# Key lookup in PEER routing: the keys written out by ScalarE before VectorE multiplies by them

## The reference, cut to what matters

```python
sv, si = lax.top_k(s, PEER_TOPK)                       # 16 best of 128, for each half
comb = sv[:, :, 0, :, None] + sv[:, :, 1, None, :]
cv, ci = lax.top_k(comb.reshape(N, PEER_HEADS, PEER_TOPK * PEER_TOPK), PEER_TOPK)
i1 = jnp.take_along_axis(si[:, :, 0], ci // PEER_TOPK, axis=-1)
i2 = jnp.take_along_axis(si[:, :, 1], ci % PEER_TOPK, axis=-1)
expert = i1 * PEER_NKEYS + i2
gate = jax.nn.softmax(cv, axis=-1)
```

## Time and profile before

| what | value |
|---|---|
| median of 3 runs | 3561.27 us (3556.86 to 3562.12) |
| time of the profiled execution | 3564.63 us |
| its span, first to last instruction | 3563.0 us |
| PE busy | 3114.4 us (87%) |
| DVE busy | 2311.0 us (65%) |
| ACT busy | 904.1 us (25%) |
| POOL busy | 1446.0 us (41%) |
| mean granted TensorE clock | 0.949 |

### The profile page before, as it was taken

One profiled execution on the slowest core, in us unless ns is written; L12 is line 12 of the kernel. 1 busy time (PEld: TensorE's weight loads), 2 busy tenths in 40 slices (PEclk: granted clock), 3 DMA queues, 4 the chain that ended last, 5 costly groups with the idle time before them and its releaser, 6 DMA issues.

```text
span 3563.0 us, 46587 instructions
## 1 busy us (share of the span) xinstructions
PE 3114.4 (87%) x17171; PEld 2346.7 (66%) x17171; DVE 2311.0 (65%) x4881; ACT 904.1 (25%) x1256; POOL 1446.0 (41%) x1188
## 2 busy tenths in 40 slices
PE   8899969444677557999999999999999999999996
PEld 1466634222454446888887888888888888888884
DVE  1233218999988976777776777776777775444445
ACT  0111111000666782222222122222222222221222
POOL 0001001555444556555554555555545543222224
PEclk9999989777899888999999999999999999999998
DMA  9611242666121329999998999999999997655654
GB/s 359 174 60 67 72 157 94 229 225 224 73 101 78 159 118 357 336 334 324 337 331 314 335 326 336 335 322 335 341 325 337 329 328 258 213 195 208 212 199 177
DMA packets 305763, 858.03 MB, mean 241 GB/s; under 512 B 25360, under 2 KB 108816, under 8 KB 303840
## 3 DMA queue, kind: packets, MB, share of 16 engines
q0 software_dynamic: 151344, 551.09, 43.0%
q1 hardware_dynamic: 154189, 305.27, 24.8%
q10 hardware_dynamic: 108, 0.22, 0.0%
HBM read 793.34 MB, written 63.15 MB: 240 GB/s over the span
## 4 chain that ended last, share of the span: by engine, by line
PE 59%; POOL 1%; issue 1%; DVE 1%; DMA 0%; ACT 0%; DVEq 0%
PE y_ps L1724 25%; PE a_ps L1705 24%; PE picked_ps L1742 7%; PE uT_ps L1692 3%; POOL shared L1446 0%; POOL rstd_d L1450 0%; DMA shared<-in_peer_u,ids 0%; POOL shared L1398 0%; POOL quad L1408 0%; DMA quad<-in_peer_v,idsT 0%; DVE h_lo L1640 0%; POOL quad L1446 0%; DVE uT_lo L1528 0%; DVE quad L1652 0%; DVE shared L1569 0%
## 5 line engine op out<-in xcount | busy, mean ns | idle before, releaser
L1408 POOL DMA_INDIRECT quad<-in_peer_v,idsT x512 | 533.4, 1042 | 518.2 <-PE picked_ps L1742 367.5
L1398 POOL DMA_INDIRECT shared<-in_peer_u,ids x384 | 444.5, 1158 | 640.5 <-DVE acts L1569 593.0
L1557 DVE TENSOR_TENSOR shared<-shared,y_ps 128x512 f32<-128x512 f32 x640 | 439.2, 687 | 340.2 <-PE y_ps L1724 312.1
L1705 PE MATMUL a_ps<-h_hi,uT_lo 128*128 128x320 f32 x2048 | 643.1, 314 | 1.7 <-DVE h_lo L1640 1.7
L1705 PE MATMUL a_ps<-h_hi,uT_hi 128*128 128x320 f32 x2048 | 633.1, 309 | 0.0
L1705 PE MATMUL a_ps<-h_lo,uT_hi 128*128 128x320 f32 x2048 | 633.1, 309 | 0.0
L1724 PE MATMUL y_ps<-v_hi,m_lo 128*128 128x512 f32 x1280 | 510.7, 399 | 11.0 <-DVE shared L1557 8.5
L1724 PE MATMUL y_ps<-v_lo,m_hi 128*128 128x512 f32 x1280 | 504.3, 394 | 0.0
L1724 PE MATMUL y_ps<-v_hi,m_hi 128*128 128x512 f32 x1280 | 501.6, 392 | 0.0
L1569 DVE CUSTOM_DVE_ANT_0 shared<-shared 128x1024 f32<-128x1024 f32 x384 | 464.6, 1219 | 22.3 <-DMA shared<-in_peer_u,ids 17.2
L1705 PEld LDWEIGHTS a_ps<-h_hi,uT_lo 128*128 128x128 f32 x2048 | 385.3, 188 | 7.2 <-issue 2.1
(11 more groups left out here) (172 smaller groups left out, 4220.1 us busy)
## 6 DMA issues: line engine op xcount, KB each, us to landing
shared<-in_peer_u SPq DMA_DIRECT2D x128, 512.0 KB
v_all<-in_peer_v SPq DMA_DIRECT2D x128, 512.0 KB
gate_blocks<-dense SPq DMA_DIRECT2D x10, 4096.0 KB, 11.7
gates<-gate_blocks SPq DMA_DIRECT2D x64, 640.0 KB
w_ada<-in_w_ada SPq DMA_DIRECT2D x12, 2048.0 KB, 11.0
x_in<-in_x_prompt SPq DMA_DIRECT2D x16, 512.0 KB, 4.1
quad<-in_peer_v,idsT POOLq DMA_INDIRECT x512
shared<-in_w_in SPq DMA_DIRECT2D x8, 768.0 KB, 12.5
```

Of the source, the lines that this page charges most:

```text
L1398: pool.indirect_dma_start(out=rows[n % 4], out_offset=None, in_=u_table, in_offset=bass.IndirectOffsetOnAxis(ap=ids[:, t, slot:slot + 1], ...
L1408: pool.indirect_dma_start(out=quads[half][q], out_offset=None, in_=v_table, in_offset=bass.IndirectOffsetOnAxis(ap=idsT[:, t, token:token ...
L1557: nc.vector.tensor_tensor(part, part, y_ps[n % RING][:, :], ALU.add).then_inc(S.y_free, 1)
L1705: last = nc.tensor.matmul(a_ps[n][:, 0:GROUP], lhs[s][:, k, :], rhs[:, k, tok], start=k == 0 and m == 0, stop=k == KD - 1 and m == 2)
```

## The change

A buffer `key_wide` is added that holds, for the eight heads of one half, each key written out 16 times. ScalarE fills it (`widen_keys`), for the first half at b = 6 and for the second half at b = 14 of the same period. VectorE multiplies by this buffer. Since both halves share one buffer, ScalarE's second filling waits for VectorE's first product (`first_keyed`), and VectorE's second product waits for the second filling. The first product now stands ahead of `rows(15)`, the second behind it. VectorE's wait behind the writing of `best_key` is dropped.

```diff
+        key_wide = sbuf(nc, mem, "key_wide", [P, HEADS, TOPK, TOPK], BF16)
...
+            def widen_keys(t, s):
+
+                act.wait_ge(S.best_key, t + 1)
+                if s:
+                    act.wait_ge(S.first_keyed, t + 1)
+                else:
+                    wait(act, S.keyed, t)
+                nc.scalar.activation(key_wide[:, :, :, :],
+                                     key4[:, :, s, :].rearrange("p h (a o) -> p h a o", o=1)
+                                     .to_broadcast([P, HEADS, TOPK, TOPK]), ACT.Copy).then_inc(S.key_wide, 1)
...
+                    if choose is not None and b == 6:
+                        widen_keys(choose, 0)
                     if choose is not None and b == 12:
                         act.wait_ge(S.shifted, choose + 1)
                         nc.scalar.activation(soft[:, :, :], soft[:, :, :], ACT.Exp).then_inc(S.exp, 1)
+                    if choose is not None and b == 14:
+                        widen_keys(choose, 1)
...
-                own.mark(nc.vector.tensor_copy(best_key[:, :, :], best_at[:, :, :]))
+                wait(dve, S.key_wide, t * 2)
+                nc.vector.tensor_copy(best_key[:, :, :], best_at[:, :, :]).then_inc(S.best_key, 1)
                 rows(3)
-                own.settle()
...
+                own.settle()
+                dve.wait_ge(S.key_wide, t * 2 + 1)
+                nc.vector.tensor_tensor(hit[:, 0:HEADS], hit[:, 0:HEADS], key_wide[:, :, :, :], ALU.mult)\
+                    .then_inc(S.first_keyed, 1)
                 rows(15)
-                own.settle()
-                for s in range(2):
-                    own.mark(nc.vector.tensor_tensor(
-                        hit[:, s * HEADS:(s + 1) * HEADS], hit[:, s * HEADS:(s + 1) * HEADS],
-                        key4[:, :, s, :].rearrange("p h (a o) -> p h a o", o=1)
-                        .to_broadcast([P, HEADS, TOPK, TOPK]), ALU.mult))
+                dve.wait_ge(S.key_wide, t * 2 + 2)
+                own.mark(nc.vector.tensor_tensor(hit[:, HEADS:HP], hit[:, HEADS:HP], key_wide[:, :, :, :], ALU.mult))
+                dve.wait_ge(S.first_keyed, t + 1)
                 own.settle()
```

More of the change, by code:

```diff
@@ L702, in routing @@
                                "scores_used shifted exp gate_ready keyed slotsT_ps slotsT left_hot left "
-                               "right_hot right place_ps placed out0 out1 dve expert picked row_in used "
+                               "right_hot right place_ps placed out0 out1 best_key key_wide first_keyed dve expert picked row_in used "
                                "u0 u1 u2 u3 u4 u5 u6 u7")
@@ L930, in _ @@
             own = Order(dve, S.dve)
-            PER_TILE = 141
+            PER_TILE = 139
             dve.wait_ge(S.iota, 2)
```

## The result

| | before | after |
|---|---|---|
| median of 6 runs, us | 3561.32 (3556.86 to 3564.86) | 3534.97 (3530.5 to 3539.57) |
| ratio to before | 1 | 0.9925, 95% interval 0.9915 to 0.9935 |
| predicted | | 3551.2 (3546 to 3559) |

The sign was right, the size was not, and the question is where the other 16 us came from. (The two profiled executions lie 31.1 us apart, spans 3563.0 and 3531.9; single executions of either kernel scatter by 8 to 9 us.)

A forecast was written before the change was run, and what follows sets the result against it. PE bounds the experts, DVE tiles 1 to 4, ACT tiles 5 to 7 from batch 4, DVE tile 8. Terms 0.1 - 8.1 - 0.3 - 1.85 = -10.1 us gave 3551.2 us, range 3546 to 3559.

The forecast's parts named there:

- Prices of products and copies: Each new product on DVE takes 1.22 us instead of 2.28, each added copy on ACT 1.9 us.
- The two rivals on them: Copies slow at 4.25 us, sum +15.9 us (chance 0.07); products stay at 2.28 us, together +8.9 us (chance 0.04).
- the slow copies: Rival on ACT's copies: 4.25 us each, sum +15.9 us, 3577 us; by the skill's rule 3.5 us each (chance 0.07).
- The two other rivals: Tiles 5 to 7 keep ACT's full 1.75 us, sum -4.5 (0.22); tiles 5 to 8 all save 2.0, sum -16 (0.05).
- Tile 0, +0.1: In tile 0 the second copy must follow the exponentials, so the first add starts 0.1 us later.
- Tiles 1 to 4, -8.1: From L1032's start to the first add 9.01 us become 7.00, 2.02 saved four times, second copy hidden by row products.
- Tiles 5 to 7, the work in them, -0.3: DVE's 2.1 us saved go into ACT's delay of 1.75 and waits for POOL: -0.1 us a tile, periods unchanged within 1 us.
- the bound of -0.85: Tiles 5 to 7: the gain if POOL is out of the way and the copy alone is waited for.
- Tile 8, -1.85: In tile 8 the comparison L1032 no longer stands behind POOL's `right`, and ACT leads: 1.85 us saved, bounds 0 and -2.0.

The follow-up runs named there:

- e3: The changed kernel with both copies and all waits kept, but the two products read best_key repeated as before: 3551.85 us, 0.9963 of before.
- e1: The kernel before with fifteen idle increments ahead of routing on VectorE, its loop moved by 14 instructions: 3544.96 us, 0.9946 of before.
- e5: The changed kernel once more, unaltered: 3536.52 us, 0.9926 of before.
- e10: The kernel before with VectorE's loop over tiles 5 to 7 written out: 3544.32 us, 0.9948 of before.
- e12: The changed kernel with the change in tiles 0 to 4 alone, the old order and repeated key in tiles 5 to 8: 3534.31 us, 0.9922 of before.
- e8: The changed kernel with its loop moved by 48 more instructions on VectorE: 0.9919 of before.
- e11: The changed kernel with VectorE's loop over tiles 5 to 7 written out: 3537.09 us, 0.9927 of before.

## Why the prediction was wrong

**The step that failed** is that for tiles 5 to 7. It took their periods as filled with the work of DVE, ACT and POOL, and said that they stay unchanged within 1 us (91.4, 93.7 and 88.0 us became 83.7, 83.7 and 83.4). They held 19.2 us of DVE at a standstill for code, and the change removed 18.5 of them by moving the loop. With about 7.5 us of its own work that makes 26.0 of the 26.4 us measured. The sum had no term for the place of the code, and no rival did; the range could not reach there. The row was in the profile of before: idle time of a `MAX8` that nothing ended. The worth of the work itself was forecast well: by the tiles below it is +0.3 - 7.3 - 2.8 = -9.8 us in the profiles, and 7.2 to 7.5 us by the times, where 10.1 was said. That the sign of the whole was right says little, since most of the gain came from what the sum did not hold.

**Prices of products and copies:** right, 1.22 and 1.95 us (1.22 and 1.9 taken). The two rivals on them fall. (For the 2.28 of the old product the overlap had to be added to the 4.49 before halving, not taken off; the figure is right, 2.29 in e3.) The 1.9 was in part luck: it was drawn through two rows as plain copies, and that of 1024 elements, `squares`, is a squaring. The rule of the Trainium skill that went with the slow copies ("Vector Engine (DVE) Microarchitecture Reference", 5.2), which the page measured on DVE, does not carry over to this copy on ACT: with each element read 16 times it took 1.89 us in tile 0, where ACT has nothing else beside it, and not 3.5.

**The two other rivals** fall by the tiles: tiles 5 to 7 do not keep ACT's whole delay (+5.3 us), and ACT's delay is not absorbed either (2.0 saved in each of tiles 5 to 8).

**Tile 0, +0.1:** +0.3 against e1, and as described: the second product waits 2.13 us for its copy, which stands behind the exponentials.

**Tiles 1 to 4, -8.1:** -7.3 against e1 (1.8, 1.8, 1.8, 2.0). The second copy is hidden by the two row products.

**Tiles 5 to 7, the work in them, -0.3:** -1.8 in the mean of the profiles above (-3.6 for the first profile against e1, -0.6 for e5's). The mechanism was as described, but for the last wait, which is ACT's copy and not POOL. End of tile 6 after, answering to the earlier trace rows:

```profile
1053.73 2.28 DVE L1048 TENSOR_TENSOR work<-rank,iota_rank 128x4096 bf16<-128x4096 bf16 x1
1054.53 3.77 POOL L840 TENSOR_TENSOR right<-right_hot,gateT 128x1024 f32<-128x1024 bf16 x1 [1.27 <-PE place_ps L1190]
1056.14 3.25 DVE L1055 TENSOR_TENSOR work<-work,key_wide 128x2048 bf16<-128x2048 bf16 x1
...
1060.06 2.76 POOL L840 TENSOR_TENSOR right<-right_hot,gateT 128x1024 f32<-128x1024 bf16 x1 [1.77 <-DVE right_hot L1102]
1060.42 2.07 ACT L889 ACTIVATE key_wide<-best_key 128x2048 bf16<-128x2048 bf16 x1
...
1062.53 1.38 DVE L1059 TENSOR_TENSOR work<-work,key_wide 128x2048 bf16<-128x2048 bf16 x1 [1.94 <-ACT key_wide L889]
```

The first product takes 3.25 with POOL in front (3.5 said). The second starts 8.80 behind the comparison's start (9.28 worked out), the copy being what ends last, not POOL: the bound of -0.85 that the prediction named. How much later ACT's first copy makes the comparison start (1.75 said) can't be read from one pair of tiles: it starts 69.5 us into tile 6 here, and 69.7 in e1. In the nine tiles 5 to 7 of e1, e10 and e12 it starts 68.0 to 69.7 us into the tile, in the twelve of the changed kernel, e5, e8 and e11 69.5 to 72.7: 1.5 later in the mean. From its start to the first add it is 10.2 us for 12.4. Together that is some -0.7 a tile.

**Tile 8, -1.85:** -0.7 in the first profile and in e5's. End of tile 8 after, answering to the earlier trace rows:

```profile
1217.09 2.39 DVE L1044 CAST rank<-ranks 128x128 bf16<-128x128 f32 x1
...
1220.61 2.28 DVE L1048 TENSOR_TENSOR work<-rank,iota_rank 128x4096 bf16<-128x4096 bf16 x1
...
1228.68 2.11 DVE L1059 TENSOR_TENSOR work<-work,key_wide 128x2048 bf16<-128x2048 bf16 x1 [1.21 <-ACT key_wide L889]
```

The comparison is free of `right` (2.28 us for 4.50), as said. But it starts 69.3 us into the tile where it was taken to start as before, at 67.7, and that is most of what is missing. It is not ACT that holds DVE there: the cast just ahead runs beside `right` of batch 13 and takes 2.39 us (0.21 before). In e8 the comparison starts 68.2 in, and the tile takes 84.30. Why DVE meets `right` at that instruction stays open. Ahead of its first add the second product then waits 1.21 us for the copy.

## What to carry to other kernels

Before pricing an edit inside or ahead of a long loop, look at the first instruction behind the loop's jump: idle time put down to "issue", with packets on an instruction queue, was code being fetched here, and 14 instructions more ahead of the loop, of whatever kind, switched it off. Judge such an edit beside a copy of the old kernel with its loop moved by as many idle instructions; else the place of the code is taken for the worth of the work (here 18.5 of 26 us). What helped here was to write the loop out for that engine, to move it, or to keep the large stores away from the jump.

## What the runs showed of the hardware

A loop of some 310 instructions on DVE was kept or fetched anew, five packets of 8 KB a round, by its place: fetched at 0 and 110 instructions from before's place, counted within 128, and kept at 14 and 62, with either kernel's work. The packets wait behind the data: 3.1 and 1.4 us a jump with quiet queues, 7.4 and 2.2 behind a store of 4 MB. Code without jumps was fetched beside the same stores with no stall above 0.2 us. A copy on ACT that reads each element 16 times took 1.89 us for 128x2048 bf16, where 1.92 had been worked out from shorter rows read once.
